# One fused encoder layer on one core: the first two weight chunks interleaved along the contraction, x issued from ScalarE's queue

## The reference

```python
proj = x @ w_in[l]                       # (512,1024) @ (1024, 7236)
(aq, ak, av, aiq, aik, aiw, bq, bk, bv, cq, ck, cv, dq, dk, dv, gate_logits) = jnp.split(proj, splits, axis=-1)
...                                      # four attentions on heads of 64, one with an indexer and top-k
y = sum_i gates[:, :, i] * (branches[i] @ w_branch[l, i])
x = layer_norm(ALPHA * x + y @ w_out[l], ln_mix_g[l], ln_mix_b[l])
hg, hu = jnp.split(x @ w_ffn_in[l], 2, axis=-1)
x = layer_norm(ALPHA * x + (jax.nn.silu(hg) * hu) @ w_ffn_out[l], ln_ffn_g[l], ln_ffn_b[l])
```

## Time and profile before

| what | value |
|---|---|
| median of 3 runs | 861.37 us |
| the profiled execution | 860.42 us |
| its span, first to last instruction | 858.6 us |
| mean granted clock of TensorE | 0.992 |
| TensorE busy | 835.9 us, 97% of the span |
| VectorE busy | 505.4 us, 59% |
| ScalarE busy | 347.7 us, 41% |

### The profile page before, as it was taken

The page is one execution under the profiler, slowest core; times in us unless marked ns, Lnnn a source line. Parts: engine busy times, 40 slices in busy tenths (PEclk is TensorE's granted clock), DMA queues, the critical chain, the costliest instruction groups (busy, mean ns, idle before and its releaser), DMA issues.

```text
span 858.6 us, 10360 instructions
## 1 busy us (share of the span) xinstructions
PE 835.9 (97%) x3975; PEld 695.9 (81%) x3975; DVE 505.4 (59%) x831; ACT 347.7 (41%) x527; POOL 31.4 (4%) x81
## 2 busy tenths in 40 slices
PE   7999999999999999999999899999999999999995
PEld 4889898888887888888888688888888888888884
DVE  4357888888788987766553686333433333322227
ACT  4545566675645546534341632222222222211112
POOL 2600000000000000000000100000000000000001
PEclk9999999999999999999999999999999999999998
DMA  6552221212121221212253123322222222222202
GB/s 221 172 198 69 80 98 53 95 50 89 59 84 64 98 82 66 97 57 92 98 201 142 50 98 126 119 98 98 98 98 98 98 98 99 98 98 98 98 0 98
DMA packets 14680, 84.50 MB, mean 98 GB/s; under 512 B 1696, under 2 KB 2724, under 8 KB 5936
## 3 DMA queue, kind: packets, MB, share of 16 engines
q1 hardware_dynamic: 12480, 76.83, 24.8%
q0 software_dynamic: 2016, 6.86, 2.4%
q10 hardware_dynamic: 144, 0.26, 0.1%
HBM read 81.82 MB, written 2.13 MB: 98 GB/s over the span
## 4 chain that ended last, share of the span: by engine, by line
PE 84%; DVE 11%; ACT 2%; issue 1%; DMA 1%; POOL 0%; SPq 0%; DVEq 0%; POOLq 0%; ACTq 0%
PE bank L1181 57%; PE bank L1352 17%; PE bank L1311 2%; DVE w_lo L786 1%; PE bank L1218 1%; PE bank L1275 1%; DVE sel L863 1%; PE bank L1277 1%; ACT w_hi L500 1%; DVE top L861 1%; PE bank L1298 1%; PE bank L1410 1%; DVE pT_lo_D L891 1%; DMA xraw<-in_xT 1%; PE bank L1204 1%
## 5 line engine op out<-in xcount | busy, mean ns | idle before, releaser
L786 DVE TENSOR_TENSOR w_lo<-raw,w_hi 128x2048 fp32r<-128x2048 f32 x68 | 155.8, 2290 | 150.4 <-ACT w_hi L500 127.7
L1181 PE MATMUL bank<-x_lo,w_hi 128*128 128x512 f32 x720 | 183.8, 393 | 0.0
L1181 PE MATMUL bank<-x_hi,w_hi 128*128 128x512 f32 x720 | 179.4, 391 | 0.0
L1181 PE MATMUL bank<-x_hi,w_lo 128*128 128x512 f32 x720 | 178.4, 389 | 0.0
L1181 PEld LDWEIGHTS bank<-x_hi,w_lo 128*128 128x128 f32 x720 | 135.0, 188 | 28.1
L1181 PEld LDWEIGHTS bank<-x_lo,w_hi 128*128 128x128 f32 x720 | 134.5, 189 | 27.2
L1181 PEld LDWEIGHTS bank<-x_hi,w_hi 128*128 128x128 f32 x720 | 134.0, 188 | 27.5 <-DVE w_lo L786 0.3
L500 ACT ACTIVATE w_hi<-raw 128x2048 fp32r<-128x2048 f32 x47 | 90.2, 1918 | 107.4 <-PE bank L1352 94.9
L1352 PE MATMUL bank<-w_hi,h_hi 128*128 128x512 f32 x176 | 56.8, 389 | 0.0
L1352 PE MATMUL bank<-w_lo,h_hi 128*128 128x512 f32 x176 | 56.8, 389 | 0.0
L1352 PE MATMUL bank<-w_hi,h_lo 128*128 128x512 f32 x176 | 56.7, 389 | 0.0
(11 more groups left out here) (279 smaller groups left out, 1054.1 us busy)
## 6 DMA issues: line engine op xcount, KB each, us to landing
raw<-in_stream SPq DMA_DIRECT2D x68, 1024.0 KB, 4.8
resid<-in_x POOLq DMA_DIRECT2D x1, 2048.0 KB, 8.2
xraw<-in_xT SPq DMA_DIRECT2D x3, 512.0 KB, 7.3
out<-result SPq DMA_DIRECT2D x3, 512.0 KB, 2.6
raw<-in_stream SPq DMA_DIRECT2D x2, 512.0 KB, 8.2
bias_b<-bias_vectors POOLq DMA_DIRECT2D x1, 1024.0 KB, 6.3
bias_a<-bias_vectors POOLq DMA_DIRECT2D x1, 1024.0 KB, 10.6
ln_g<-in_g POOLq DMA_DIRECT2D x2, 512.0 KB, 7.7
```

The lines of the kernel that those rows point to most:

```text
L786: dve.tensor_tensor(w_lo[:, s, :], raw[:, s, :], w_hi[:, s, :].bitcast(f32), ALU.subtract).then_inc(lo_ready, 1)
L1181: ins = pe.matmul(dst, lhs[a](k), rhs[b](k), start=n == 0, stop=n == n_all - 1)
```

## The change

Chunk 0 and chunk 1 are loaded together, in six pieces along k: four single ones and two pairs. A piece holds the same k of both chunks, all 256 columns. ScalarE issues the six pieces of x on its own queue, ahead of its table load. For each piece it copies the 4 columns, waits for that copy, makes the high part of both chunks in one instruction (in the last piece in two), and makes the high part of x. TensorE does, for each k, nine matmuls: three parts for each of three banks (`first_chunks`). Chunk 2 now comes in two halves with a high and a low part for each half; SyncE issues the halves when pieces of chunk 0 are free, and ScalarE's high parts wait for `tile_done` of the first bank (`wait_used(act, 0)`). Slot 2 waits for both halves. The calls for chunk 2 at t = 1 go, and counts of semaphores move by one.

```diff
-PIECES = [(0, 1), (1, 2)] + [(k, k + 2) for k in range(2, KT, 2)]
+PIECES = [(k, k + 1) for k in range(KT // 2)] + [(k, k + 2) for k in range(KT // 2, KT, 2)]
...
         def _(sp):
             for i, (k, end) in enumerate(PIECES):
-                sp.dma_start(by_tile(raw, 0)[:, k:end, 0:CVW],
-                             stream[0].rearrange("p (k n) -> p k n", k=KT)[:, k:end, 0:CVW]).then_inc(first_loaded[i], 16)
-                sp.dma_start(xraw[:, k:end, :], xT[:, k:end, :]).then_inc(x_loaded[i], 16)
+                s = slice(CW * k, CW * end)
+                sp.dma_start(raw[:, :, s], stream[0:2, :, s].rearrange("c p n -> p c n")).then_inc(first_loaded[i], 16)
             half = CHUNK_COLS // 2
-            sp.dma_start(raw[:, 1, 0:half], stream[1, :, 0:half]).then_inc(second_loaded, 16)
-            sp.dma_start(raw[:, 1, half:], stream[1, :, half:]).then_inc(raw_loaded[1], 16)
+            sp.wait_ge(first_lo_ready, KT // 2)
+            sp.dma_start(raw[:, 0, 0:half], stream[2, :, 0:half]).then_inc(half_loaded, 16)
+            sp.wait_ge(first_lo_ready, len(PIECES))
+            sp.dma_start(raw[:, 0, half:], stream[2, :, half:]).then_inc(raw_loaded[0], 16)
+            sp.wait_ge(lo_ready, 1)
+            sp.dma_start(raw[:, 1, :], stream[3]).then_inc(raw_loaded[1], 16)
...
+            for i, (k, end) in enumerate(PIECES):
+                act.dma_start(xraw[:, k:end, :], xT[:, k:end, :]).then_inc(x_loaded[i], 16)
             act.preload_act_table_set("natural_log_exp_and_others")
             for i, (k, end) in enumerate(PIECES):
+                s = slice(CW * k, CW * end)
                 act.wait_ge(first_loaded[i], 16)
-                act.activation(by_tile(w_hi, 0)[:, k:end, 0:P], by_tile(raw, 0)[:, k:end, 0:P], ACT.Copy).then_inc(first_hi_ready, 1)
+                step(act.activation(by_tile(raw, 1)[:, k:end, HEAD:HEAD + HEADS], by_tile(raw, 0)[:, k:end, P:P + HEADS], ACT.Copy))
+                step_wait()
+                if end < KT:
+                    act.activation(w_hi[:, :, s], raw[:, :, s], ACT.Copy).then_inc(first_hi_ready, 1)
+                else:
+                    act.activation(w_hi[:, 0, s], raw[:, 0, s], ACT.Copy).then_inc(first_hi_ready, 1)
+                    act.activation(w_hi[:, 1, s], raw[:, 1, s], ACT.Copy).then_inc(hi_ready, 1)
                 act.wait_ge(x_loaded[i], 16)
                 act.activation(x_hi[:, k:end, :], xraw[:, k:end, :], ACT.Copy).then_inc(x_hi_ready, 1)
-            for half, loaded, ready in ((0, second_loaded, second_hi_ready), (1, raw_loaded[1], hi_ready)):
...
+            for half, loaded, ready in ((0, half_loaded, half_hi_ready), (1, raw_loaded[0], hi_ready)):
+                s = slice(CHUNK_COLS // 2 * half, CHUNK_COLS // 2 * (half + 1))
                 act.wait_ge(loaded, 16)
+                wait_used(act, 0)
+                act.activation(w_hi[:, 0, s], raw[:, 0, s], ACT.Copy).then_inc(ready, 1)
             empty_tile(0, 0)
...
-            for half, hi, lo in ((0, second_hi_ready, second_lo_ready), (1, hi_ready, lo_ready)):
+            for half, hi, count, lo in ((0, half_hi_ready, 1, half_lo_ready), (1, hi_ready, 2, lo_ready)):
                 s = slice(CHUNK_COLS // 2 * half, CHUNK_COLS // 2 * (half + 1))
-                dve.wait_ge(hi, 1)
-                dve.tensor_tensor(w_lo[:, 1, s], raw[:, 1, s], w_hi[:, 1, s].bitcast(f32), ALU.subtract).then_inc(lo, 1)
+                dve.wait_ge(hi, count)
+                dve.tensor_tensor(w_lo[:, 0, s], raw[:, 0, s], w_hi[:, 0, s].bitcast(f32), ALU.subtract).then_inc(lo, 1)
...
+            def first_chunks():
+                tiles = [columns(0, 0, P, CW), columns(1, 0, P, CW), columns(1, P, P, CW)]
                 for k in range(KT):
                     piece = next(i for i, (_, end) in enumerate(PIECES) if k < end)
                     pe.wait_ge(first_lo_ready, piece + 1)
+                    if piece == len(PIECES) - 1:
+                        pe.wait_ge(lo_ready, 1)
                     pe.wait_ge(x_lo_ready, piece + 1)
+                    for g, w in enumerate(tiles):
                         for n, (a, b) in enumerate(PARTS):
+                            ins = pe.matmul(prod[g][:], w[a](k), x_all[b](k), start=k == 0 and n == 0,
                                             stop=k == KT - 1 and n == len(PARTS) - 1)
                         if k == KT - 1:
                             ins.then_inc(tile_done, 1)
...
+                if t == 2:
+                    pe.wait_ge(half_lo_ready, 1)
                 pe.wait_ge(lo_ready, t)
```

More of the change, by code:

```diff
@@ L375, in _ @@
             for i, (k, end) in enumerate(PIECES):
-                sp.dma_start(by_tile(raw, 0)[:, k:end, 0:CVW],
-                             stream[0].rearrange("p (k n) -> p k n", k=KT)[:, k:end, 0:CVW]).then_inc(first_loaded[i], 16)
-                sp.dma_start(xraw[:, k:end, :], xT[:, k:end, :]).then_inc(x_loaded[i], 16)
+                s = slice(CW * k, CW * end)
+                sp.dma_start(raw[:, :, s], stream[0:2, :, s].rearrange("c p n -> p c n")).then_inc(first_loaded[i], 16)
             half = CHUNK_COLS // 2
-            sp.dma_start(raw[:, 1, 0:half], stream[1, :, 0:half]).then_inc(second_loaded, 16)
-            sp.dma_start(raw[:, 1, half:], stream[1, :, half:]).then_inc(raw_loaded[1], 16)
-            with sp.Fori(2, N_CHUNKS - 1, 2) as c:
-                for j in range(2):
[L385 to L390, removed]
+            sp.wait_ge(first_lo_ready, KT // 2)
[4 more added lines that the diff above has]
+            sp.dma_start(raw[:, 1, :], stream[3]).then_inc(raw_loaded[1], 16)
+            with sp.Fori(4, N_CHUNKS - 1, 2) as c:
+                for j in range(2):
+                    sp.wait_ge(lo_ready, c - 2 + j)
                     sp.dma_start(raw[:, j, :], stream[bass.ds(c + j, 1)].rearrange("a p n -> p (a n)")).then_inc(raw_loaded[j], 16)
@@ L422, in _ @@
             pool.wait_ge(x_loaded[-1], 16)
-            pool.wait_ge(raw_loaded[1], 16)
+            pool.wait_ge(half_loaded, 16)
             pool.dma_start(t5_sb[:], t5T).then_inc(tables_loaded, 16)
@@ L496, in high @@
                 s = c % 2
-                act.wait_ge(raw_loaded[s], 16 * ((c + 1) // 2))
+                act.wait_ge(raw_loaded[s], 16 * (c // 2))
                 if c >= 2:
@@ L663, in _ @@
                     unit_stage2(before)
-                high(t + 1)
+                if t > 1:
+                    high(t + 1)
                 if t == INDEX_SLOT - 1:
@@ L749, in ffn_pair @@
                 else:
-                    high_of(FIN0 + 1 + 2 * p, (FIN0 + 1) % 2, p + (FIN0 + 2) // 2, up_done, 2 * p)
+                    high_of(FIN0 + 1 + 2 * p, (FIN0 + 1) % 2, p + (FIN0 + 1) // 2, up_done, 2 * p)
                 for j in range(2):
@@ L755, in ffn_pair @@
                     act.activation(swi[:, j, :], banks[4 * parity + j][:], ACT.Tanh, scale=0.5).then_inc(tanh_ready, 1)
[L756 removed]
+                high_of(FIN0 + 2 + 2 * p, FIN0 % 2, p + (FIN0 + 2) // 2, gate_done, 2 * p + 2)
                 for j in range(2):
@@ L972, in _ @@
             for i, (k, end) in enumerate(PIECES):
+                s = slice(CW * k, CW * end)
                 dve.wait_ge(first_hi_ready, i + 1)
-                dve.tensor_tensor(by_tile(w_lo, 0)[:, k:end, 0:P], by_tile(raw, 0)[:, k:end, 0:P],
-                                  by_tile(w_hi, 0)[:, k:end, 0:P].bitcast(f32), ALU.subtract).then_inc(first_lo_ready, 1)
+                if end < KT:
+                    dve.tensor_tensor(w_lo[:, :, s], raw[:, :, s], w_hi[:, :, s].bitcast(f32), ALU.subtract).then_inc(first_lo_ready, 1)
+                else:
+                    dve.tensor_tensor(w_lo[:, 0, s], raw[:, 0, s], w_hi[:, 0, s].bitcast(f32), ALU.subtract).then_inc(first_lo_ready, 1)
+                    dve.wait_ge(hi_ready, 1)
+                    dve.tensor_tensor(w_lo[:, 1, s], raw[:, 1, s], w_hi[:, 1, s].bitcast(f32), ALU.subtract).then_inc(lo_ready, 1)
                 dve.wait_ge(x_hi_ready, i + 1)
@@ L1000, in _ @@
                 elif kind is None or kind == "D":
-                    low(t + 1)
+                    if t > 1:
+                        low(t + 1)
                 if t in (INDEX_SLOT, INDEX_SLOT + 1):
@@ L1201, in first_chunk @@
                     pe.wait_ge(first_lo_ready, piece + 1)
+                    if piece == len(PIECES) - 1:
+                        pe.wait_ge(lo_ready, 1)
                     pe.wait_ge(x_lo_ready, piece + 1)
[L1203 to L1216, removed]
+                    for g, w in enumerate(tiles):
                         for n, (a, b) in enumerate(PARTS):
-                            ins = pe.matmul(prod[TILE0[1] + j][:], w[a](k), x_all[b](k), start=k == 0 and n == 0,
+                            ins = pe.matmul(prod[g][:], w[a](k), x_all[b](k), start=k == 0 and n == 0,
                                             stop=k == KT - 1 and n == len(PARTS) - 1)
@@ L1318, in _ @@
```

(3 more changed lines are left out.)

8 lines of the change are left out of this document (1 added, 7 removed).

## The result

The changed kernel took 863.02 us (median of 19 runs, 860.98 to 865.69) against 861.03 us (median of 19, 858.48 to 862.35) for the kernel before. The ratio is 1.002, 95% interval 1.0013 to 1.0026: slower by 0.2%, some 1.7 us. I had forecast 860.5, with a range from 858.4 to 862.8, and put 0.51 on a difference too small to tell. The profiled execution took 862.55 us, its span is 860.8 us, 2.2 more than before.

The account below looks back on a forecast made before the run. TensorE, busy 97% of the span, bounds the kernel; only the head can give. Slot 2 earlier by 2.4 us and a clock fall of 1.5 make -0.9: from 861.37 to 860.5 us, range 858.4 to 862.8.

Parts of the forecast that it names:

- the new wait: Ahead of slot 2, TensorE waits for chunk 2's parts: 2.3 us idle, slot 2 at E + 2.5.
- E: Time at which the 72 matmuls of chunks 0 and 1 end in issue on TensorE, forecast 23.8 us.
- The fall of the clock behind it: Behind the gap ahead of slot 2, granted clock 0.50 for some 3 us, costing 1.5 us, at most 1.7.
- The whole stretch behind slot 2: From slot 2 to the kernel's end: whatever time slot 2 begins earlier is carried to the end.
- the sum -2.4 + 1.5: Whole kernel: slot 2 starts 2.4 us earlier, a clock fall costs 1.5 us, together -0.9 us.
- The data: Head loads: 4.2 MB at 260, then 390 GB/s; single pieces at 4.0 to 10.0, double ones at 12.7 and 15.4.
- I take 0.3, since weights are issued as early as x here: Head, at k = 4: TensorE stands 0.3 us for the first double piece, out of a possible 0 to 1.3.
- TensorE starts at about 7.2: Start of the head: after ScalarE's six issues, table load and piece 0's parts, first real matmul near 7.2 us.
- rival (b): Head: TensorE's start and pieces late, rows of 1 KB at 200 GB/s, slot 2 at 29.6, 863.0 us; chance 0.18.
- The 24 matmuls of the first chunk: Head of the kernel before: 24 matmuls, 18 shown in the chain, said to run after TensorE's start at 11.93.

## Why the prediction was wrong

**Right in mechanism and size:** the new wait. Forecast E + 2.5 for slot 2 and 2.3 us idle; measured 2.34 idle and 29.45 - 26.95 = 2.50, with E one step behind the last start at 26.72. The fall of the clock behind it (forecast 1.5, at most 1.7) came, and with the gap filled it was gone together with some 2 us. The whole stretch behind slot 2 kept its length within the falls of the clock, as forecast. In the sum -2.4 + 1.5 the first term measured +0.8, and the second, in the profiled pair, +1.4. That the second fits so well is in part luck: the fall near 262 went and another near 491 came.

**The step that failed: "The data", and in it the sentence "I take 0.3, since weights are issued as early as x here".** It made k = 4 begin at 15.4 + 0.3 = 15.7, with the first double piece landed at 12.7. It landed at 14.86, was through both engines at 18.56, and k = 4 began at 18.70. That is 3.0 of the 3.15 us by which the start of slot 2 was missed (29.45 against 26.3). My rate was not wrong: from 2 to 12 us I had 2.1 MB and then 2.0 us at 390 GB/s, 2.9 MB, and 308 GB/s over 10 us are 3.1 MB. What was wrong is the idea that bytes land in the order in which they are wanted. I divided a total rate over the pieces one after the other, and with x on its own queue they do not come so: the same rate on one queue had the same piece there at 12.15. With one queue the schedule of the prediction even holds: weights at 4.0, 6.0, 8.0, 10.0 and 12.7 in the forecast, ScalarE at them at 3.63, 6.03, 7.41 (there without a wait), 10.19 and 12.15. It was a schedule for the queue that the change gave up. The kernel before with x moved alone shows the same lateness of the weights.

**The term that was too small: "TensorE starts at about 7.2".** It began at 8.70 in the profiled execution after, and at 7.54 in the one with another bank order, whose head is the same. The issues took 3.1 us in the latter (forecast 2.8) and 4.3 in the former; the fifth and sixth became long, as rival (b) had it. Of itself this cost nothing in the changed kernel: with the warm-up lengthened and no fall in the head, k = 4 was still not begun before 19.11. It would have bound if the pieces had come in time.

**What I left out of the sum:** that a gap ahead of the first matmul also brings the clock down. It did at 9.7, for 3.4 us. Again hidden by the late k = 4.

**The rivals.** Rival (b), slower by a late start and late pieces, is what happened: k = 4 at 18.9 was its number, 18.70 the measurement. I gave it 0.18, because I tied it to rows of 1 KB running at 200 GB/s. The right arrival had a wrong reason. Its end (E = 27.1, slot 2 at 29.6) is within 0.2 us of the trace. Its 863.0 is the measured median, but by luck: it is the middle between its two cases, and with the fall that came its own sum gives 863.8. The Trainium skill, page "DMA: Bandwidth & Descriptors", section "Issuing engines are not separate DMA queues", says that DMAs of all issuing engines share the same 16 DMA engines and interleave. The trace agrees in the rate (308 against 309 GB/s). I used the half of the rule that says nothing is gained, and not the half that says they interleave, from which the order of landing follows to be in doubt.

**Smaller slips.** The 24 matmuls of the first chunk did not all start at 11.93: six of them (k = 0 and 1) ran from 5.67 and 6.92, and the 18 of the chain are the rest. The terms of the start add up to 7.1, not 7.2. And the range was said to hold (b) "without its worst", but its upper end, 862.8, lies below (b)'s own middle, 863.0.

**What stays open:** why two queues land the wanted piece 2 to 3 us later at the same rate. That x runs ahead of the weights fits the kernel before with x moved, but not the kernel with pieces by turns. One rival is untested: with two queues all issues were made by 3.9 to 5.1 us, with one only by 7.7 to 8.8, and no run has two queues and a slow issue, so the pace is not told from the number of queues. No run followed the 16 DMA engines one by one. Single executions differ by a fall of the clock (some 1.4 us) either way, so the profiles tell of mechanisms, the medians of sizes.

## What to carry to other kernels

When loads feed a pipeline in order, cost the time at which each piece is complete, not the bytes over the rate: a second queue did not raise the rate here and made the piece that was wanted next late. Before an operand buffer is shared by an interleaved loop, ask when its last reader ends: the interleave moved that to the end of the loop, and finishing two of the three banks early took away all of the wait. A gap on TensorE can bring the clock down and then costs more than its length, here 2.3 us and some 1.4 on top, so a reordering that keeps the engine busy can be worth more than the gap shows.

## What the runs showed of the hardware

A DMA issue on ScalarE took 0.44 to 0.56 us at first, not far from SyncE's 0.40 to 0.50, but the last of a burst took up to 1.45, and with twelve in a row the eleventh 1.18 (on SyncE up to 1.67). While they run, nothing behind them on ScalarE starts. The rate has a dip in the changed kernel too: 158 GB/s from 6 to 8 us between 326 before it and 311 behind it, and 147 with the other bank order. These have no rows of 528 bytes, to which I had put the 140 GB/s of the earlier trace rows, so such rows are not needed for it; what makes the dip stays open. In the head of the eleven profiled executions every gap of 2.0 us or more on TensorE (2.02 to 2.68, and 4.06, 4.14 and 5.98) went with 3.4 us or more at the lower clock, and none of 1.76 or less did. Later in the kernel the length alone does not decide. The gap near 260 lasts 1.95 to 2.03 us in all eleven; the clock fell behind it in three (behind 2.03, 1.95 and 1.96) and not in eight, among them one of 2.02. The gap that ends between 482 and 491 lasts 1.76 us in all eleven, and the clock fell behind it in five.
